# Attention in a hybrid transformer layer: TensorE issues both maps' scores of step i+2 ahead of step i's transposes

## What is computed

```python
def diff_attention(q, k, v, lam, g_head, lambda_init):
    def blk(i, qb):
        s = jnp.einsum('bqhmd,bkhmd->bhmqk', qb, k).astype(jnp.float32) * scale
        p = jax.nn.softmax(s, axis=-1)
        a = p[:, :, 0] - lam * p[:, :, 1]
        return jnp.einsum('bhqk,bkhe->bqhe', a.astype(v.dtype), v)
...
def sink_attend(qb, k, v, sink, mask):
    s = jnp.einsum('bqngd,bknd->bngqk', qb, k) * (B_HEAD_DIM ** -0.5)
    if mask is not None:
        s = jnp.where(mask, s, NEG_INF)
    p = jax.nn.softmax(jnp.concatenate([s, sk], axis=-1), axis=-1)[..., :-1]
    return jnp.einsum('bngqk,bknd->bqngd', p.astype(v.dtype), v)
```

## Time and profile before

| | us |
|---|---|
| median of 3 runs | 1444.0 |
| lowest, highest | 1435.49, 1444.94 |
| the profiled execution | 1434.05 |
| its span, first to last instruction | 1432.2 |
| PE busy | 1240.4 |
| DVE busy | 869.5 |
| ACT busy | 682.7 |

### The profile page before, as it was taken

The page is one execution under the profiler, slowest core; times in us unless marked ns, Lnnn a source line. Parts: engine busy times, 40 slices in busy tenths (PEclk is TensorE's granted clock), DMA queues, the critical chain, the costliest instruction groups (busy, mean ns, idle before and its releaser), DMA issues.

```text
span 1432.2 us, 16864 instructions
## 1 busy us (share of the span) xinstructions
PE 1240.4 (87%) x5963; PEld 976.6 (68%) x5963; DVE 869.5 (61%) x952; ACT 682.7 (48%) x768; POOL 316.9 (22%) x285
## 2 busy tenths in 40 slices
PE   2689999997999998989563699999999999999951
PEld 0567787775565666878452588888888888888741
DVE  1353132123667653352336599999999999999846
ACT  2232233123233333213221488877777877777732
POOL 3022031000001000110320133333333333333200
PEclk9899999997678997999855799999999999999985
DMA  9434335551000000342013699999999999999924
GB/s 304 157 117 152 114 117 203 194 203 67 0 1 1 1 1 15 110 150 93 0 73 120 219 367 379 377 374 364 360 356 357 362 359 366 362 361 358 358 92 192
DMA packets 144844, 292.15 MB, mean 204 GB/s; under 512 B 11953, under 2 KB 13106, under 8 KB 144146
## 3 DMA queue, kind: packets, MB, share of 16 engines
q1 hardware_dynamic: 127986, 259.06, 50.7%
q0 software_dynamic: 14688, 28.12, 5.9%
q10 hardware_dynamic: 2112, 4.19, 0.8%
HBM read 286.48 MB, written 27.92 MB: 220 GB/s over the span
## 4 chain that ended last, share of the span: by engine, by line
PE 66%; DVE 11%; ACT 7%; issue 7%; DMA 6%; POOL 1%; ACTq 0%; POOLq 0%; SPq 0%; DVEq 0%
PE psum L1042 17%; PE psum L1044 16%; PE psum L1043 16%; DVE w_lo L1750 3%; DMA pt<-gates_scratch 2%; PE psum L1172 2%; DMA ada_first<-in_w_ada 2%; PE psum L1180 2%; ACT w_hi L962 2%; PE psum L1209 2%; PE psum L1228 2%; PE psum L1060 2%; PE psum L1300 1%; PE psum L1222 1%; ACT L979 1%
## 5 line engine op out<-in xcount | busy, mean ns | idle before, releaser
L1042 PE MATMUL psum<-w_hi,act_hi 128*128 128x512 f32 (+1 forms) x1288 | 513.0, 398 | 25.9 <-DVE w_lo L1409 15.1
L1044 PE MATMUL psum<-w_hi,act_lo 128*128 128x512 f32 (+1 forms) x1288 | 500.2, 388 | 0.0
L1043 PE MATMUL psum<-w_lo,act_hi 128*128 128x512 f32 (+1 forms) x1288 | 499.1, 388 | 0.0
L1042 PEld LDWEIGHTS psum<-w_hi,act_hi 128*128 128x128 f32 x1288 | 243.3, 189 | 96.0 <-DVE w_lo L1409 15.7
L1044 PEld LDWEIGHTS psum<-w_hi,act_lo 128*128 128x128 f32 x1288 | 243.0, 189 | 51.1
L1043 PEld LDWEIGHTS psum<-w_lo,act_hi 128*128 128x128 f32 x1288 | 243.7, 189 | 45.2
L1750 DVE TENSOR_TENSOR w_lo<-raw_extra,w_hi 128x2048 fp32r<-128x2048 f32 x96 | 217.3, 2290 | 45.4 <-ACT w_hi L962 45.4
L1750 DVE TENSOR_TENSOR w_lo<-raw_mix,w_hi 128x2048 fp32r<-128x2048 f32 x96 | 218.9, 2289 | 12.2 <-ACT w_hi L962 12.2
L962 ACT ACTIVATE w_hi<-raw_mix 128x2048 fp32r<-128x2048 f32 x96 | 183.7, 1916 | 26.7 <-PE psum L1044 26.7
L962 ACT ACTIVATE w_hi<-raw_extra 128x2048 fp32r<-128x2048 f32 x96 | 180.7, 1913 | 5.8 <-PE psum L1044 5.8
L1409 DVE TENSOR_TENSOR w_lo<-raw_mix,w_hi 128x2048 fp32r<-128x2048 f32 (+1 forms) x26 | 57.3, 2207 | 176.2 <-ACT w_hi L797 176.2
(11 more groups left out here) (244 smaller groups left out, 1256.7 us busy)
## 6 DMA issues: line engine op xcount, KB each, us to landing
raw_mix<-in_w_e SPq DMA_DIRECT2D x96, 1024.0 KB, 8.4
raw_extra<-in_w_e SPq DMA_DIRECT2D x96, 1024.0 KB, 8.5
raw_mix<-in_w_in SPq DMA_DIRECT2D x16, 1024.0 KB, 6.2
raw_mix<-in_w_ada SPq DMA_DIRECT2D x16, 1024.0 KB, 7.2
gates_scratch<-rows POOLq DMA_DIRECT2D x20, 256.0 KB, 2.7
pt<-gates_scratch POOLq DMA_DIRECT2D x20, 256.0 KB, 3.7
ada_first<-in_w_ada ACTq DMA_DIRECT2D x4, 1024.0 KB, 19.8
ada_first<-in_w_ada SPq DMA_DIRECT2D x4, 1024.0 KB, 20.4
```

The costliest lines, as they stand in the source:

```text
L1042: pe.matmul(out, a_hi(ka_), w_hi[:, kw, :], start=s, stop=False)
L1043: pe.matmul(out, a_hi(ka_), w_lo[:, kw, :], start=False, stop=False)
L1044: ins = pe.matmul(out, a_lo(ka_), w_hi[:, kw, :], start=False, stop=e)
```

## The change

In every step the scores of both maps of step i+2 are issued before the transposes of step i, instead of map 0 behind the first group and map 1 behind the second. The wait for the exponentials of step i moves with them. Nothing is added or removed, and the other engines' lists stay as they are.

```diff
@@ -1199,6 +1199,9 @@
                 kind, tile, h, _, nk, vt, q = steps[i]
                 b = i % 2
                 w = nk * P
+                if i + 2 < NSTEP:
+                    scores(i + 2, 0)
+                    scores(i + 2, 1)
                 for j, g in enumerate(groups(i)):
                     n = use_no[("p", i, j)]
                     if j == 0:
@@ -1208,10 +1211,6 @@
                     for x, kt in enumerate(g):
                         ins = pe.transpose(bank(6)[:, x * P:(x + 1) * P], src[:, kt * P:(kt + 1) * P], ident[:, :])
                     ins.then_inc(pt_done, 1)
-                    if i + 2 < NSTEP:
-                        scores(i + 2, j)
-                if len(groups(i)) == 1 and i + 2 < NSTEP:
-                    scores(i + 2, 1)
                 for j in range(len(groups(i))):
                     wait_emptied(pe, use_no[("p", i, j)])
```

## The result

The changed kernel takes 1536.99 us (median of 4 runs, 1534.77 to 1546.01), the kernel before 1440.28 beside it (1435.49 to 1444.94). The ratio is 1.068, with a 95% interval of 1.062 to 1.075: 97 us slower, where 1540 was forecast. The profiled execution has a span of 1536.5 us, 104.3 more than before. The mean granted clock of each of the four runs, 0.841 to 0.857, shows that the profiled one (0.848) is a usual one; 30 runs of the kernel before, taken later beside the experiments, have 0.902 to 0.915.

A forecast was written before the change was run, and what follows sets the result against it. TensorE, busy nearly always in attention, was taken as the bound. Windowed +69, differential +30 and context +2 made +101 on 1434.05 us, 1535; with half the median's excess, 1540 us. Range 1505 to 1562, down to 1455 if only waits are paid.

The forecast's parts named there:

- The two waits: TensorE idles before second transposes and before values: 0.86 and 0.45 us per differential step, 0.86 and 0.76 per four-block windowed step.
- The overlapped pair of scores: Differential steps: both maps' scores, standing together, overlap on different halves of the array's rows, giving back 0.4 us at 2.4 GHz.
- The windowed steps: Windowed attention steps: clock low until the merge, 158 us against 89, so +69 us, containing +15 for waits.
- The differential steps: Differential latent steps: +30 us with the clock mixed, between +6 with the clock as now and +47 low throughout.
- The context tile: Context tile, 8 steps with one group of transposes each: +2 us.
- The clock in the windowed steps: TensorE's clock falls to 1.2 GHz in the first windowed steps and stays down until the merge.
- Rival B: All attention steps: the clock stays as it is and only the waits are paid, +23 us, 1457 us; chance 0.17.
- The falls in the trace of before: Attention in the kernel before: TensorE's clock falls stand behind waits of about 2 us.
- The allowance of 5 us: Whole kernel: half of the 10 us by which the runs' median lay above the profiled execution, added to 1535.
- two rules of the Trainium skill: TensorE's clock: lost by long idle gaps (1457 us), or made to swing by frequent micro-idles; the prediction leaned on the second.

The follow-up runs named there:

- run 7: Kernel before with extra products in differential flush waits and the last steps' waits, map 0 ahead only in steps 26, 30, 34: 1421.53 us, ratio 0.992.
- run 2: Kernel before with the new order only from step 24 on, the windowed steps: 1519.66 us, ratio 1.057.
- run 3: Changed kernel with extra unread TensorE products filling both waits of each windowed step: 1483.79 us, ratio 1.033.
- run 4: Kernel before with 9 extra products behind output transposes at each of four differential flushes: 1432.89 us, ratio 0.995; the profiled execution took 1499.70.
- run 1: Kernel before with the new order only in steps 0 to 23, the windowed steps in the old order: 1459.92 us, ratio 1.018.

## Why the prediction was right

The time, the sign and the mechanism came out as forecast; the terms were each off by some microseconds.

- *The two waits.* Forecast 0.86 and 0.45 us in a differential step, measured 0.79 and 0.46. In a windowed step 0.86 and 0.76 against 0.78 and 0.73 to 0.78. They were read from rows in which the same copies were hidden, and that held; the first wait stands in all 32 steps, with 25.1 us in all. (401.89 + 0.05 - 400.56 is 1.38, not 1.39.)
- *The overlapped pair of scores.* Seen in one row at 1.2 GHz (4.20 us for x8) and halved for 2.4 GHz: a gain of 0.4. Measured at 2.4 GHz 397.00 - 394.76 = 2.24 us against 2 x 1.27 (the start-to-start of 401.09 and 402.36): 0.3. The plain differential step became 5.76 us long; in the old order one without any wait takes 4.55 (run 7, 395.39 to 399.94). So 1.2 was lost per step, not 0.9. The two waits less the pair's gain are 0.95 of it; the rest is spread over the two groups of transposes and the values, which take 0.06 to 0.13 us more each than without waits.
- *The windowed steps.* Forecast +69, measured +77.9. The period with four blocks was priced at 11.3 and is 11.8, and the 16 steps at 158 us take 162.4. Besides, I took the transposes at 474.9 for the first of the windowed steps; they are those of the last differential step, and the stretch of before is 84.5, not 89. Each of the two makes half of the error of 9.
- *The differential steps.* Forecast +30 between ends of +6 and +47; measured +16.5, the largest error of a term. (The upper end has the same slip: 16 steps priced at 148 us stand against 104.5, which makes +43.) The clock came back more often than I assumed: its mean over these steps is 0.71 (0.79 before), not near 0.50. The guess that the pair right behind the values might bring it up is not shown by itself, since values and output transposes also meet at a flush.
- *The context tile.* Forecast +2, measured +5.5, of which about 4 is the shifted pair of scores.
- *The clock in the windowed steps,* on which all hangs. That it would fall and stay down was argued from falls behind waits and rises behind values with full transposes. Run 2 shows the fall from full clock in the first step, run 3 shows that filling the waits brings it back, run 4 that the clock alone costs 58 us. One detail differs: in the changed kernel the clock was already down at 486.9 us, in the last differential step but one, 15 us ahead of the first windowed transposes. There the new order kept it from coming back (run 1 against it); that it also brings it down within the windowed steps is shown by run 2 and not by the changed kernel. Rival B (1457, only the waits) had the waits about right: it priced them at 15 us in the windowed steps, and run 4 against the changed kernel puts them at 20.
- *The falls in the trace of before.* The prediction says that they stand behind waits of about 2 us. That is so for three of the five in attention (413.8, 444.5, 468.4). The first, at 393.3 us, stands behind two shorter ones:

```profile
388.95 0.63 PE L1209 MATMUL psum<-ident,rows 128*128 128x128 f32 x4 [0.88 <-DVE rows L484]
391.65 0.33 PE L1209 MATMUL psum<-ident,rows 128*128 128x128 f32 x1 [0.80 <-DVE pt L1615]
```

The last, at 553.8 us, came during a wait of 1.36 behind one of 0.87. Single waits of 0.88 to 0.94 us in the windowed steps (before 488.30 and 509.63) brought no fall. So the trace of before already had a case much like the new order, two waits of under 1 us within one step, and the clock fell from 2.4 GHz behind it. Read closely, that row would have been firmer ground for the main term than the context tile, which never was at 2.4 GHz.

- *The allowance of 5 us* for the median above the profiled execution was not needed: the changed kernel's median lies 1.3 below its profiled time of 1538.26, and further runs of before lie at 1435 to 1436, near the 1434.05 from which the sum began.

Of the two rules of the Trainium skill ("TensorE: Matmul & The Clock Gate") that were weighed, the one on frequent micro-idles (section on PSUM-queue depth-cycling) fits this case, and the one on long gaps (section on HAM oscillation) does not: waits of 0.5 to 0.8 us were enough. But the section on depth-cycling speaks of swinging between the two levels, and in the windowed steps the clock did not swing; the third row of the changed kernel has it at 1.2 GHz for 184 us.

The sum came out nearer than its terms deserve, and that is luck: -14 in one stretch and +9 and +3 in others cancel.

## What to carry to other kernels

When TensorE's row has no waits, work placed between an operation and its copy-out is a cover; moving it ahead opens waits that are short but come in every step. Price them, then ask in which state of the clock the row was: a stretch that holds 2.4 GHz can fall to 1.2 GHz by two waits of under 1 us per step, and here the clock then cost about three times what the waits did (58 and 20 us). A busy share of 85 to 95% hides this; the granted clock by stretch and the length of one known matmul show it, and a few matmuls that nobody reads, put into the waits, test it in one run.

## What the runs showed of the hardware

- The clock can stay down through a stretch in which TensorE is busy 95% of the time: 152.45 of 160.40 us in run 4, in the old order, without a rise. In the same steps it stays at 2.4 GHz for 75 to 79 us if it entered so (run 1, the kernel before). The windowed steps in the old order were seen to keep either level.
- The clock fell from 2.4 GHz behind two waits within one step, of 0.78 and 0.52 us (run 2, at 492.4 us) and of 0.88 and 0.80 us (the kernel before, at 393.3 us).
- Work that yields nothing made a kernel faster: 53 us in run 3, 13 us together with one reordering in run 7.
- Matmuls over 64 rows in the two halves of the array overlapped when issued next to each other: 2.24 us for a pair that takes 2.54 apart at 2.4 GHz, 4.13 against 4.86 at 1.2 GHz (472.94 to 477.07 in the changed kernel; all from start to start). The last piece of map 1, which shares a PSUM bank with map 0, waits until map 0 is done; whether more would overlap without that wait was not tried.
